# RWKV recurrence in a fused ten-phase kernel: norm-weight rows moved to the project phase, masks in two halves with the row half first, keys behind the masks, scores issued ahead of sums

## What is computed

```python
mod = silu(c) @ ada_w[0] + ada_b[0]                 # 6 x 1024 numbers
sh1, sc1, g1, sh2, sc2, g2 = split(mod, 6)
h = rms(x) * (1 + sc1) + sh1
y = rwkv7_mix(h, ...)                               # phases project, chunks, output
x = x + g1 * y
h = rms(x) * (1 + sc2) + sh2                        # used by the fourth phase, the FFN
# rwkv7_mix, per head of 64 and per token:
sa    = state @ a_t
state = state * w_t + sa b_t^T + v_t k_t^T
y_t   = state @ r_t
```

## Time and profile before

| | us |
|---|---|
| median of 3 runs (2782.47 to 2784.24) | 2783.05 |
| the profiled execution's own time | 2777.63 |
| its span | 2775.8 |
| PE busy | 2558.0 (92%) |
| DVE busy | 1209.3 (44%) |
| ACT busy | 979.5 (35%) |
| POOL busy | 965.2 (35%) |
| project phase, until the first instruction of the chunks on DVE | 238.4 |
| chunks phase, until its last sum on POOL | 485.5 |

### The profile page before, as it was taken

One profiled execution on the slowest core, in us unless ns is written; L12 is line 12 of the kernel. 1 busy time (PEld: TensorE's weight loads), 2 busy tenths in 40 slices (PEclk: granted clock), 3 DMA queues, 4 the chain that ended last, 5 costly groups with the idle time before them and its releaser, 6 DMA issues.

```text
span 2775.8 us, 33779 instructions
## 1 busy us (share of the span) xinstructions
PE 2558.0 (92%) x14024; PEld 1990.0 (72%) x14024; DVE 1209.3 (44%) x1797; ACT 979.5 (35%) x1446; POOL 965.2 (35%) x334
## 2 busy tenths in 40 slices
PE   7996676789999989998999999989899999999999
PEld 6754565268887867876888778869587777777686
DVE  5565885864443262343111442434307424344604
ACT  4652444232322233533332332222324334333523
POOL 2312222224444433443344434314433333222232
PEclk8998899799999998999999999999999999999999
DMA  6122442224555322122224332202122222111121
GB/s 260 61 76 50 97 86 77 100 74 182 192 194 197 136 77 75 46 76 76 98 99 159 131 138 91 91 33 101 42 91 91 80 91 91 61 46 61 38 91 61
DMA packets 91957, 272.11 MB, mean 98 GB/s; under 512 B 54704, under 2 KB 54832, under 8 KB 64304
## 3 DMA queue, kind: packets, MB, share of 16 engines
q1 hardware_dynamic: 88944, 252.94, 25.8%
q10 hardware_dynamic: 2880, 17.30, 1.6%
HBM read 264.44 MB, written 5.78 MB: 97 GB/s over the span
## 4 chain that ended last, share of the span: by engine, by line
PE 77%; DVE 11%; ACT 5%; issue 3%; DMA 3%; POOL 2%; ACTq 0%; SPq 0%; DVEq 0%; POOLq 0%
PE bank L343 19%; PE bank L345 19%; PE bank L344 19%; PE bank L279 2%; PE bank L278 2%; PE bank L277 2%; PE bank L3169 1%; PE bank L2644 1%; DMA gain_weights<-in_gains 1%; DVE conv_out L2370 1%; POOL ring_low L374 1%; ACT w_high L364 1%; PE bank L2890 1%; PE bank L3157 1%; DVE probs L3366 1%
## 5 line engine op out<-in xcount | busy, mean ns | idle before, releaser
L374 POOL TENSOR_TENSOR ring_low<-ring,w_high 128x2048 fp32r<-128x2048 f32 (+2 forms) x184 | 800.1, 4350 | 1347.9 <-ACT w_high L364 1347.9
L343 PE MATMUL bank<-h_high,w_high 128*128 128x512 f32 (+1 forms) x1304 | 523.2, 401 | 28.0 <-DVE h_low L454 20.0
L345 PE MATMUL bank<-h_high,ring_low 128*128 128x512 f32 (+1 forms) x1304 | 519.4, 398 | 0.0
L344 PE MATMUL bank<-h_low,w_high 128*128 128x512 f32 (+1 forms) x1304 | 517.8, 397 | 0.0
L364 ACT ACTIVATE w_high<-ring 128x2048 fp32r<-128x2048 f32 (+2 forms) x184 | 330.9, 1801 | 373.6 <-PE bank L345 356.5
L343 PEld LDWEIGHTS bank<-h_high,w_high 128*128 128x128 f32 (+1 forms) x1304 | 247.1, 190 | 94.8 <-issue 27.3
L345 PEld LDWEIGHTS bank<-h_high,ring_low 128*128 128x128 f32 (+1 forms) x1304 | 246.2, 189 | 60.7
L344 PEld LDWEIGHTS bank<-h_low,w_high 128*128 128x128 f32 (+1 forms) x1304 | 246.3, 189 | 59.7 <-issue 0.7
L343 PE MATMUL bank<-z_high,w_high 128*128 128x512 f32 x384 | 153.7, 400 | 10.5 <-DVEq L1875 4.4
L345 PE MATMUL bank<-z_high,ring_low 128*128 128x512 f32 x384 | 153.3, 399 | 0.0
L344 PE MATMUL bank<-z_low,w_high 128*128 128x512 f32 x384 | 152.3, 397 | 0.0
(11 more groups left out here) (442 smaller groups left out, 4455.1 us busy)
## 6 DMA issues: line engine op xcount, KB each, us to landing
ring<-in_stream SPq DMA_DIRECT2D x194, 1024.0 KB, 4.8
ada_slot<-in_ada_next SPq DMA_DIRECT2D x40, 512.0 KB, 3.3
ada_slot<-in_first SPq DMA_DIRECT2D x8, 1024.0 KB, 5.4
gain_weights<-in_gains ACTq DMA_DIRECT2D x4, 2048.0 KB, 13.6
scale_weights<-in_first SPq DMA_DIRECT2D x4, 1024.0 KB, 19.2
inverse<-scratch_inverse SPq DMA_DIRECT2D x16, 256.0 KB, 4.1
g_weights<-in_gains ACTq DMA_DIRECT2D x2, 2048.0 KB, 15.0
w_first<-in_first SPq DMA_DIRECT2D x2, 1024.0 KB, 7.9
```

What stands on the lines that cost most here:

```text
L343: pe.matmul(out, w_high[:, k, cols], x_high, start=start, stop=False)
L344: pe.matmul(out, w_high[:, k, cols], x_low, start=False, stop=False)
L345: return pe.matmul(out, w_low[:, k, cols], x_high, start=False, stop=stop)
L374: pool.tensor_tensor(self.c.ring_low[:, b % SLOTS, 0:cols], self.c.ring[:, b % SLOTS, 0:cols], self.high_buf[:, b % 2, 0:cols].bitcast(F32 ...
```

## The change

1. The 16 tiles of norm-weight rows leave the chunks phase. DVE now does them in the project phase, behind the low parts of k and ahead of the mixes w, a, v, g. Their rows are loaded in 8 transfers of 1 MB into two buffers that lie where `v_mix` lies. Two transfers are issued early, four behind the load of b_k + 3, two behind the next load; each from the third on waits for the two tiles that free its buffer. ACT waits for the last of the 16 tiles before it writes the first part of the v mix.
2. A mask instruction of 4 x 128 columns becomes two of 4 x 64. The four of the row half come first and have a semaphore of their own, on which POOL's levels and SP's row transfer now wait.
3. The keys of pair n + 1 are formed behind the masks of pair n, a turn ahead of their scores.
4. PE issues the scores of pair n behind outer and ahead of the sums of pair o. On ACT the growth factors for the keys move ahead of the evictions of the sums.

```diff
@@ rwkv_project
+    late_w = chip.over("late_weights", [P, 2, SLOT], F32, xx_offset)
...
             if n == 1 or n == 3:
                 split.high(act, b_k + 2 + n // 2)
+                if n == 1:
+                    act.wait_ge(late_sum.sem, late_sum.of(2 * KD - 1))
                 for k in range(4 * (n // 2), 4 * (n // 2) + 4):
                     mix("v", k)
...
         rest("k", KD - 1)
+        for i in range(KD):
+            dve.wait_ge(late_in[i % 2].sem, late_in[i % 2].of(16 * (i // 2) + 15))
+            for j in range(2):
+                ada_tile(chip, dve, late_w[:, i % 2, j * D:(j + 1) * D], 3 * KD + 2 * i + j).then_inc(late_sum.sem, 1)
+        dve.wait_ge(late_sum.sem, late_sum.of(2 * KD - 1))
+        ada_finish(chip, dve, 3 * KD, 5 * KD, biased, one_plus)
         for s in "wavg":
...
+        def late(i):
+            if i < 2:
+                sp.wait_ge(mean.sem, mean.of(0))
+            else:
+                sp.wait_ge(late_sum.sem, late_sum.of(2 * i - 3))
+            sp.dma_start(late_w[:, i % 2, :], chip.io["first"][6 + i]).then_inc(late_in[i % 2].sem, 16)
         for b in range(b_r, chip_end):
             chip.load(sp, b)
+            if b < b_r + 2:
+                late(b - b_r)
+            elif b == b_k + 3:
+                for i in range(2, 6):
+                    late(i)
+            elif b == b_wa:
+                late(6)
+                late(7)
@@ rwkv_chunks, PE
             outer(q, 0)
             outer(q, 1)
+
+        def sums(q):
             u_out.wait(pe, q)
...
                 scores(n, 0)
                 scores(n, 1)
+            if C:
+                sums(o)
+            if A:
                 masked.wait(pe, n)
@@ rwkv_chunks, DVE
-            for part in range(2):
-                for h in range(2):
-                    s_mm.wait(dve, n, 2 * part + h)
-                    dve.tensor_tensor(SC[n % 3][:, h, 4 * part:4 * part + 4, CHUNK:3 * CHUNK],
...
+            for done, half in ((low_masked, 1), (masked, 0)):
+                cols = slice((1 + half) * CHUNK, (2 + half) * CHUNK)
+                for part in range(2):
+                    for h in range(2):
+                        s_mm.wait(dve, n, 2 * part + h)
+                        dve.tensor_tensor(SC[n % 3][:, h, 4 * part:4 * part + 4, cols],
...
+        key(0)
         for p in range(-1, KD + 2):
...
             if A:
-                key(n)
                 mask(n)
+            if n + 1 < KD:
+                key(n + 1)
...
-            if solves:
-                next_ada(p)
@@ rwkv_chunks, POOL and SP
-            masked.wait(pool, p)
+            low_masked.wait(pool, p)
...
-            masked.wait(sp, p)
+            low_masked.wait(sp, p)
```

More of the change, by code:

```diff
@@ L745, in rwkv_project @@
     split_v = Split(chip, b_v, 4, offset=h_offset)
+    late_w = chip.over("late_weights", [P, 2, SLOT], F32, xx_offset)
+    late_in = [Step(chip, f"rw_late_in{n}", 8 * KD) for n in range(2)]
+    late_sum, biased, one_plus = Step(chip, "rw_late_sum", 2 * KD), Step(chip, "ada_biased", 1), Step(chip, "ada_one_plus", 1)
     c_in, vec_in, const_in = (Load(chip) for _ in range(3))
@@ L1177, in rwkv_chunks @@
     UV = [chip.keep(f"u_v_{n}", [P, NC_, 2, CHUNK]) for n in range(2)]
-    ada_slot = chip.over("ada_slot", [P, SLOT], F32, chip.ring_offset)
-    spare = chip.ring_offset + 4 * SLOT
+    spare = chip.ring_offset
     SC.append(chip.over("scores_2", [P, 2, NC_, 3 * CHUNK], F32, spare))
@@ L1199, in rwkv_chunks @@
     grown, kept, keyed = per("grown", 2), per("kept", 1), per("keyed", 4)
-    s_mm, masked = per("s_mm", 4), per("masked", 4)
+    s_mm, low_masked, masked = per("s_mm", 4), per("low_masked", 4), per("masked", 4)
     bk_mm, bk_out = per("bk_mm", 2), per("bk_out", 2)
@@ L1454, in scalar @@
                            .then_inc(w_out.sem, 1)
+            if n + 1 < KD:
+                grow(n + 1)
+            if C:
                 no_mm.wait(act, o, 0)
@@ L1566, in solve_corner @@
             dve.tensor_copy(square(sub[:, 0, :]), y_all.rearrange("p m j -> p j m")).then_inc(solved.sem, 1)
[L1568 to L1571, removed]
         def merge(q, mm, out, dst, old, first):
@@ L1582, in mask @@
                 no_mm.wait(dve, n - 3)
-            for part in range(2):
-                for h in range(2):
-                    s_mm.wait(dve, n, 2 * part + h)
-                    dve.tensor_tensor(SC[n % 3][:, h, 4 * part:4 * part + 4, CHUNK:3 * CHUNK],
-                                      bank(4 + 2 * part + h, P),
-                                      chip.k("causal").unsqueeze(1).to_broadcast([P, 4, P]), ALU.mult)\
-                       .then_inc(masked.sem, 1)
+            for done, half in ((low_masked, 1), (masked, 0)):
[4 more added lines that the diff above has]
+                        dve.tensor_tensor(SC[n % 3][:, h, 4 * part:4 * part + 4, cols],
+                                          bank(4 + 2 * part + h, P)[:, :, half * CHUNK:(half + 1) * CHUNK],
+                                          chip.k("causal")[:, half * CHUNK:(half + 1) * CHUNK].unsqueeze(1)
+                                          .to_broadcast([P, 4, CHUNK]), ALU.mult).then_inc(done.sem, 1)
+        key(0)
         for p in range(-1, KD + 2):
@@ L1645, in vector @@
                 dve.tensor_tensor(part(new, g), part(Tm, g), decay_of(g, c), ALU.mult).then_inc(state.sem, 1)
-        ada_sum.wait(dve, KD - 1)
-        ada_finish(chip, dve, 3 * KD, 5 * KD, ada_biased, ada_one_plus)
     def gpsimd(pool):
         for p in range(KD):
-            masked.wait(pool, p)
+            low_masked.wait(pool, p)
             if p >= 2:
@@ L1706, in turn @@
                          .rearrange("b (i t) -> b i t", t=CHUNK)[:, :, 0:16]).then_inc(rows_in.sem, 16)
-            if p:
-                ada_sum.wait(sp, p - 1)
-            sp.dma_start(ada_slot[:, :], chip.io["first"][6 + p]).then_inc(ada_in.sem, 16)
         turn(0)
@@ L1732, in sync @@
                 turn(p + 1)
-        ada_sum.wait(sp, KD - 1)
         gr_mm.wait(sp, KD - 3)
```

4 lines of the change are left out of this document (removed).

## The result

The changed kernel takes 2817.31 us (median of 4 runs, 2813.05 to 2818.84). The kernel before took 2783.11 beside it. The ratio is 1.0119, 95% interval 1.0105 to 1.0133: slower, as forecast, and 1.3 us from the 2816 of the prediction.

The account below looks back on a forecast made before the run. The project phase was taken as PE-bound nearly throughout, the chunks phase as bound by a loop with two nearly equal paths; 15 + 21.8 - 3.8 - 0.4 = +32.6 on 2783.05 gave 2816, range 2794 to 2823.

Parts of the forecast that it names:

- The tiles in the project phase: Project phase: ACT's wait for tiles and POOL's wait for the mixes delay b_k + 3 from 150.3 to 165.3, +15.
- The rival that POOL gets in between the mixes: Project phase: POOL waits for one mix instruction only, project +6.5, in all +24, 2807; chance 0.15.
- the rival that the hole covers the tiles: Project phase: last tile ends before 122, b_k + 3 not late, project -3, in all +15, 2798; chance 0.06.
- The turns: Chunks phase: masks wait for sums, keys and levels alternate, +21.6 over turns 2 to 5; turn 6 without keys +0.2.
- Keys are cut: Chunks turns: DVE's keys behind the masks alternate with POOL's levels; keys end at C + 14.9, blocks at C + 19.65.
- The rival that they are not cut: Chunks turns: DVE holds the port over four keys; chunks +0.2, in all +15, 2798; chance 0.15.
- the one in which DVE bounds the turns: Chunks phase: each of 8 turns loses its tiles' 4.2 us, -34 against +15, -19 in all, 2764; chance 0.08.
- Early turns: Chunks turns 0 and 1: earlier row transfers, -3.2 in turn 1's path; turn -1 +1.3 as keys meet levels; together -3.8.
- Turn 7: Last chunks turn: the removed tiles' end was near the x1 merge, -0.4.
- The sum: Whole kernel: 15 + 21.8 - 3.8 - 0.4 = +32.6, giving a forecast of 2816.

Follow-up runs that it names:

- Kernel 4: Changed kernel, but ACT forms the first four parts of v, with its wait for the tiles, behind the high part of b_k + 3: 2798.24 us.
- kernel 7: Changed kernel with 17 products of the identity, which nobody reads, on PE in front of x1 in turns 2 to 5: 2814.79 us.
- kernel 5: Changed kernel, but POOL cuts its levels only when the four keys of the turn are formed: 2808.33 us.
- kernel 1: Changed kernel's project phase with its tiles, but turns in the order of before (whole masks, sums ahead of scores, keys before their masks), without tiles: 2795.32 us.
- kernel 2: As kernel 1, but with the masks in halves, row half first: 2797.71 us.
- kernel 10: As kernel 2, with ACT's wait for the tiles behind the split of b_k + 3 and 12 unread products between scores and transposes: 2769.79 us.
- kernel 8: Changed kernel, but the four row-half masks no longer wait for the sums of pair n - 3, only for the product reading that half: 2794.79 us.
- kernel 11: Changed kernel with the edits of kernel 4 and kernel 8, plus a second key buffer so keys are formed ahead of the masks: 2771.17 us.

## Why the prediction was right, and where a term was off

*The tiles in the project phase, +15*: right by every link, and 14.5 in the trace. Last tile ended 131.8 forecast, 131.3 in the trace; POOL asked at 138.8 and 138.25; ended 152.4 and 152.0; b_k + 3 ended 165.3 and 165.2. Kernel 4 shows that the cause is the place of ACT's wait. The rival that POOL gets in between the mixes fell: it waited from 138.25 to the end of the row of mixes. So did the rival that the hole covers the tiles, which had them end before 122; kernel 4 shows that they need not end sooner for the loss to go. The Trainium skill ("SBUF — State Buffer", section "Who interferes with whom") has the port held for one instruction; for this row of SCALAR_TENSOR_TENSOR the 13.71 of POOL speak against that, for the keys and levels the 1.75 agree. Why POOL gets in between two keys and not between two mixes, no run varied.

*The turns, +21.6 in turns 2 to 5 and +0.2 in turn 6*: the mechanism was right, the size was not. The trace has +27.2 and +1.4. Against the forecast by point of the turn, in turn 5: first mask C + 7.0 (forecast 5.7), keys ended C + 15.4 (14.9), `r_add` C + 16.1 (15.6), blocks C + 21.4 (19.65). Two terms were mis-sized by TensorE's clock. Scores and sums were taken at 2.06 and 3.05, from a kernel in which PE ran them at full clock; at the 0.69 to 0.74 granted here they took 2.6 and 4.1, and the masks start 1.3 late. Part of that came back, since a key that meets a level costs 1.69 from start to start, not 1.94: the keys end 0.5 late. Turns 2 and 4 are like turn 5 (C + 6.8 and C + 6.9); in turn 3 the clock stayed up behind the same wait of 2.06, the scores took 2.06, and the first mask stands at C + 5.5. And x1 was taken at 1.15 and took 1.97, y1 behind it likewise: from `r_add` to blocks it is 5.3 in place of 4.05. x1 took 1.97 in all four turns, and kernel 7 gave back 1.1 of that in turns 2 to 4. In turn 6 the scores took 2.06; there the transposes and the small products behind them ran at a granted 0.60, and x1 started 3.4 behind the transposes, where it was 2.2 before. The prediction had priced the lower clock behind the long stall of the project phase (1.7 us there), and had not asked the same of the shorter waits that its own account put into each turn: 2.06 in front of the scores, 4.19 in front of x1.

*Keys are cut*: right. They alternate with the levels at 1.75, and kernel 5 restores 0.69. The rival that they are not cut fell, and so did the one in which DVE bounds the turns (kernel 1).

*Early turns, -3.8*: -2.2, -3.5 and +0.7 in turns 0, 1 and -1, so -5.0 in all; the keys in turn -1 cost less than forecast, and turns 0 and 1 gained 0.3 more each. *Turn 7*: -0.4, as forecast.

*The sum*: +32.6 forecast, +37.7 in the traces for the two phases, +34.2 in the medians. That the time came out within 1.3 us is in part luck: turns 2 to 5 cost 5.6 more and turn 6 1.2 more than forecast, the early turns 1.2 less, and the traces' difference is 3.5 above the medians' even without what lies behind the chunks. What makes that 3.5 is open. The clock differs from turn to turn in one kernel (28.6 to 30.1 in turns with the same work), so two executions can differ by as much.

## What to carry to other kernels

Before work is moved into a hole of one engine, look at who waits for its end and what is queued behind that waiter: here the hole was free, and one wait placed in front of a split instead of behind it cost some 20 us of the phase in the traces (252.9 against 233.0) and 16 in the medians, each over the kernel before beside it (34.2 against 18.1). A semaphore wait should cover only the part of a buffer that its readers read; splitting an instruction brings its first half forward only where no wait holds that half that it doesn't need: in kernels 2 and 10 none did, in the changed kernel one did, and kernel 8 took it away. And when an edit makes PE wait longer in a loop of short bursts, price what comes behind the wait at the lower clock, then count the edit's gain.

## What was not expected of the hardware

The granted clock falls behind quite short waits of PE in the chunks phase: to 0.57 behind one of 2.17, to 0.74 behind one of 2.06, to 0.52 behind one of 4.19, while it stayed at 1.00 behind one of 1.77. The length of a wait alone doesn't decide it: behind 2.09 the scores took 2.06 (kernel 8, turn 4), behind 2.07 they took 2.99 (kernel 11, turn 5), and behind 2.89 in front of the transposes it stayed at 1.00 in turn 5 of the changed kernel and was 0.60 in turn 6. That makes turns with the same work 1.3 to 1.5 us longer or shorter, and hides small edits. Products that nobody reads, put into such a wait, kept x1 at 1.15; they held nothing up where they ended before the wait did, and put x1 2.1 us later where they didn't.
